# Who stores the moved squares of a hybrid attention layer, and a second place for them in the sparse branch

## The reference

```
h = rmsnorm(x, norm_g);  proj = h @ w_in          # (1024, 1024) @ (1024, 9.5 thousand columns)
ya = forgetting_attention(qa, ka, va, log_f) * silu(za)     # A: 8 heads, logits + c[t] - c[s], causal
yb = dsa_attention(qb, k, v, q_idx, k_idx, w_idx) * silu(zb)  # B: 8 heads share k and v; top 256 keys per query
yc = dilated_attention(qc, kc, vc) * silu(zc)               # C: 12 heads, windows with dilation 1, 4, 16
merged = sigmoid(ga) * (ya @ w_a) + sigmoid(gb) * (yb @ w_b) + sigmoid(gc) * (yc @ w_c)
out = rmsnorm(x + merged @ w_o, final_g)
```

## Time and profile before

| | before |
|---|---|
| time, median of 3 runs | 1370.05 us (1369.61 to 1372.65) |
| profiled execution, its own time | 1370.07 us |
| its span, first to last instruction | 1368.3 us |
| mean granted TensorE clock | 0.997 of full speed |
| TensorE busy | 1331.6 us (97%) |
| DVE, ACT, GpSimd busy | 771.8 (56%), 627.7 (46%), 297.3 us (22%) |

### The profile page before, as it was taken

How to read it: one execution, slowest core, us unless ns; L and a number is a source line. 1 busy time by engine, 2 the same in 40 slices (tenths; PEclk the granted TensorE clock), 3 DMA queues, 4 the chain that set the end, 5 groups by cost and what they waited for, 6 DMA issues and landing times.

```text
span 1368.3 us, 20758 instructions
## 1 busy us (share of the span) xinstructions
PE 1331.6 (97%) x7690; PEld 1084.3 (79%) x7690; DVE 771.8 (56%) x1716; ACT 627.7 (46%) x1381; POOL 297.3 (22%) x464
## 2 busy tenths in 40 slices
PE   7999999999999999999999899899999999999998
PEld 6988877777788888887778677777878788888886
DVE  6569866666766875575545454644444354223634
ACT  7467866666644541114343464544444322113223
POOL 3123111102103000005354412434342330000100
PEclk9999999999999999999999999999999999999999
DMA  7055222212214322225555423433443452321522
GB/s 223 23 139 131 63 69 63 63 44 66 70 42 124 91 68 79 81 78 156 151 144 161 137 86 94 120 83 92 133 140 100 145 155 62 84 78 62 185 92 101
DMA packets 124548, 139.54 MB, mean 102 GB/s; under 512 B 13888, under 2 KB 99520, under 8 KB 124192
## 3 DMA queue, kind: packets, MB, share of 16 engines
q0 software_dynamic: 26624, 80.00, 19.3%
q1 hardware_dynamic: 97824, 58.22, 15.7%
HBM read 99.95 MB, written 34.03 MB: 98 GB/s over the span
## 4 chain that ended last, share of the span: by engine, by line
PE 80%; DMA 7%; DVE 4%; POOL 4%; issue 3%; ACT 2%; POOLq 0%; ACTq 0%; DVEq 0%
PE bank L1120 20%; PE bank L1122 20%; PE bank L1121 20%; PE bank L1293 5%; DMA square_scratch<-pa 4%; PE slot L1254 4%; PE bank L1266 3%; PE slot L1120 2%; PE slot L1121 2%; PE slot L1122 2%; POOL ptsa L1038 2%; DVE idle_out L1673 1%; PE slot L1228 1%; DVE slot L1866 1%; DMA ptsb<-square_scratch 1%
## 5 line engine op out<-in xcount | busy, mean ns | idle before, releaser
L1120 PE MATMUL bank<-hs,w_hl 128*128 128x512 f32 x1088 | 432.7, 398 | 5.0 <-DVE qc L1809 2.9
L1122 PE MATMUL bank<-hs,w_hl 128*128 128x512 f32 x1088 | 424.6, 390 | 0.0
L1121 PE MATMUL bank<-hs,w_hl 128*128 128x512 f32 x1088 | 424.2, 390 | 0.0
L1120 PEld LDWEIGHTS bank<-hs,w_hl 128*128 128x128 f32 x1088 | 204.7, 188 | 50.6 <-issue 10.4
L1122 PEld LDWEIGHTS bank<-hs,w_hl 128*128 128x128 f32 x1088 | 204.5, 188 | 44.2
L1121 PEld LDWEIGHTS bank<-hs,w_hl 128*128 128x128 f32 x1088 | 204.9, 188 | 39.6
L1646 DVE TENSOR_TENSOR w_hl<-w_raw,w_hl 128x512 fp32r<-128x512 f32 (+1 forms) x168 | 113.3, 678 | 213.6 <-ACT w_hl L1357 212.0
L1357 ACT ACTIVATE w_hl<-w_raw 128x512 fp32r<-128x512 f32 (+1 forms) x168 | 104.0, 623 | 157.9 <-PE bank L1122 150.1
L1673 DVE TENSOR_SCALAR_CACHE_REDUCE idle_out<-score,state 128x768 uint8<-128x768 f32 (+3 forms) x140 | 115.4, 824 | 4.8
L1038 POOL DMA_DIRECT2D ptsb<-square_scratch x96 | 61.8, 650 | 119.9 <-PE bank L1293 96.0
L1866 DVE CUSTOM_DVE_ANT_0 slot<-slot,score 128x128 f32<-128x128 f32 (+5 forms) x64 | 47.0, 785 | 50.5 <-PE slot L1254 50.3
(11 more groups left out here) (337 smaller groups left out, 2439.1 us busy)
## 6 DMA issues: line engine op xcount, KB each, us to landing
w_raw<-in_w_in_dram SPq DMA_DIRECT2D x136, 256.0 KB, 2.9
merged_scratch<-ms POOLq DMA_DIRECT2D x16, 512.0 KB, 3.5
ms<-merged_scratch POOLq DMA_DIRECT2D x16, 512.0 KB, 4.1
square_scratch<-pb POOLq DMA_DIRECT2D x20, 256.0 KB, 2.9
ptsb<-square_scratch POOLq DMA_DIRECT2D x80, 64.0 KB, 2.3
xn<-in_x_dram SPq DMA_DIRECT2D x8, 512.0 KB, 6.8
iq_st<-iq_hl POOLq DMA_DIRECT2D x32, 128.0 KB, 2.8
w_raw<-in_w_o_dram SPq DMA_DIRECT2D x16, 256.0 KB, 3.3
```

What stands on the lines that cost most here:

```text
L1120: pe.matmul(out_, wh, mh, start=start, stop=False)
L1121: pe.matmul(out_, wh, ml, start=False, stop=False)
L1122: return pe.matmul(out_, wl, mh, start=False, stop=stop)
```

## The change

The store of a square is issued by ACT, behind the second exponential of the same run, with its two waits (for the transposition, and for the loads of two squares before). GpSimd keeps the four loads and the wait for the store. PTQ in B gets a second place, 512 columns of `c_tables`, so that the loads there too wait for PV of two squares back. The count of landed loads, `square_in`, is split into one for each parity of the square, and the waits on it are rewritten to match.

```diff
-                at = len(squares) - (2 if br == "a" else 1)
+                at = len(squares) - 2
...
-        PTQ = {"a": [at(k, f"ptsa{k}", [P, TB, P]) for k in (44, 76)], "b": [at(46, "ptsb", [P, 4, P])] * 2}
+        PTQ = {"a": [at(k, f"ptsa{k}", [P, TB, P]) for k in (44, 76)], "b": [at(46, "ptsb", [P, 4, P])]}
...
+        PTQ["b"].append(c_tables[:, 0:4 * P].rearrange("p (b c) -> p b c", c=P))
...
-        single_exp, squared, square_stored, square_in = sem("single_exp"), sem("squared"), sem("square_stored"), sem("square_in")
+        single_exp, squared, square_stored = sem("single_exp"), sem("squared"), sem("square_stored")
+        square_in = [sem(f"square_in{i}") for i in range(2)]
...
 # GpSimd, step "square"
-                    pool.wait_ge(squared, n + 1)
-                    if n >= 2:
-                        pool.wait_ge(square_in, 64 * (n - 1))
-                    pool.dma_start(mid[0:W // P].rearrange("b p c -> p b c"),
-                                   PR[br][:, 0, 0:W].rearrange("p (b c) -> p b c", c=P)).then_inc(square_stored, 16)
                     if a["before"] is not None:
                         full(pool, a["before"]["pv"])
                     pool.wait_ge(square_stored, 16 * (n + 1))
                     for j in range(4):
...
-                                       ).then_inc(square_in, 16)
+                                       ).then_inc(square_in[n % 2], 16)
...
 # TensorE, step "pv"
-                            pe.wait_ge(square_in, 64 * (a["square"] + 1))
+                            pe.wait_ge(square_in[a["square"] % 2], 64 * (a["square"] // 2 + 1))
...
 # ACT, at the end of step "exp"
+                    if a["dma"]:
+                        n, br, W = a["square"], a["br"], len(a["moved"]) * P
+                        act.wait_ge(squared, n + 1)
+                        if n >= 2:
+                            act.wait_ge(square_in[n % 2], 64 * (n // 2))
+                        act.dma_start(square_dram[n % 2][0:W // P].rearrange("b p c -> p b c"),
+                                      PR[br][:, 0, 0:W].rearrange("p (b c) -> p b c", c=P)).then_inc(square_stored, 16)
```

## The result

The changed kernel takes 1353.70 us (median of 4 runs, 1353.31 to 1354.19), the kernel before, beside it on the same chip, 1371.10 us (1369.61 to 1372.65). The ratio is 0.9873, 95% interval 0.9856 to 0.9890. The forecast was 1358.5 us with a range of 1354 to 1366, so the direction was right and the gain larger than forecast, by a little more than the range allowed.

What follows compares the result with a forecast made beforehand. TensorE, busy 1331.6 of 1368.3 us, was taken as the bound, leaving its idle time and lost clock to win. Gains 6.2 + 5.6 + 2.9 less 3.0 gave 11.7 us: 1358.5 us from 1370.07, range 1354 to 1366.

Steps and rivals of the forecast that it cites:

- Part 1: Stores leave GpSimd's queue, where loads stood ahead; TensorE's waits in A go: 6.2 us won.
- Rival (a): In A, stores lose in landing what they win in issue: 1364.6 us; chance 0.25 together with rival (d).
- Part 2: Start of B: first store no longer behind six share loads; less idle time, no low clock: 5.6 us won.
- The wait under "issue": TensorE's wait at the start of B, placed at 852.10 on the first product with moved blocks: 1.2 us, goes.
- The wait for yb: TensorE's wait at the start of B for the copy that frees a bank: 2.8 us, some 1.4 remain.
- The clock's 3.0 us: Start of B: granted clock no longer falls to 0.50, which cost half of 5.93 us of busy time.
- rival (d): Start of B: low clock stays, yb wait keeps its length: 1362.8 us; chance 0.25 together with Rival (a).
- Part 3: B: loads wait for PV of two squares back; four TensorE waits for loads go: 2.9 us won.
- Rival (b): Waits only move; yb copy, qa copies and ACT's issues eat the gain: 1370 us; chance 0.09.
- Part 4: ACT pays 0.37 us for each of 41 issues; TensorE sees a quarter to a fifth: 3 us lost.
- its lower bound, in brackets: ACT's cost per store issue could be 0: the sequencer might issue while the exponential still runs.
- Rival (c): ACT's issue is on the path, TensorE sees all 41: slower, 1388 us at GpSimd's 0.79 us; chance 0.05.

Runs made afterwards that it cites:

- Experiment 3: Changed kernel with ACT's stores in A only, B as in the kernel before: 1362.83 us, ratio 0.9951.
- experiment 9: Changed kernel, but in A GpSimd issues the stores, each ahead of the loads of the square before: 1353.11 us, ratio 0.9881.
- experiment 4: Changed kernel with only the first store of B back on GpSimd, behind the six loads of shares: 1359.27 us, ratio 0.9925.
- experiment 8: Changed kernel with ACT's store ahead of the second exponential instead of behind it: 1364.43 us, ratio 0.9968.
- experiment 5: Changed kernel with one more 8 KB DMA, which nothing waits for, issued by ACT behind each of 41 stores: 1355.86 us, ratio 0.9901.
- Experiment 1: Changed kernel with one place for the moved blocks of B, as before: 1356.76 us, ratio 0.9907.
- experiment 2: Second place for B alone, against the kernel before, stores still issued by GpSimd: 1366.85 us, ratio 0.9978.
- Experiment 10: Changed kernel with one extra 8 KB DMA per square issued by ACT right behind the first exponential: 1354.07 us, ratio 0.9883.
- Experiments 5 and 6: Changed kernel with one or three extra 8 KB DMAs issued by ACT behind each store: 1355.86 us with one, 1371.13 us with three.

## Why the prediction was wrong in size and right in kind

- **Part 1, 6.2 us in A: right, 6.8.** Experiment 3 gives 6.8 alone. The waits for the exponentials went, that for ptsa fell from 2.7 to 0.6. The prediction kept the landing at 5.3 us; landings fell by a quarter (4.7 to 3.5 us at 448 KB). It had named the loads ahead of the store as what counts, and experiment 9 shows just that; that the order alone, on GpSimd, does it was not among its theories. Rival (a), that what is won in issue is lost in landing, had the sign of this effect wrong.
- **Part 2, 5.6 us at the start of B: right, 6.15.** It was one store behind six loads (experiment 4 gives 5.6 to 6.0 by itself). The wait under "issue" went (it ends at 853.69; 852.10 is the start of the matmul ahead of it), and the granted clock is 1.00. The wait for yb fell from 2.8 to 0.6 us and not to 1.4. The clock's 3.0 us were sized right, and rival (d) is out. That the clock would not fall with 1.4 us of idle time left was argued from one row, where 2.7 us left it at 1.00; in experiment 8 it is low behind 2.0 us. So the row was no safe guide, though the conclusion held: in experiment 5 the yb wait is 1.3 us, and the clock shows no fall there.
- **Part 3, 2.9 us for the second place: right, about 3.** Experiment 1, without it, loses 3.0 us at two places. Behind the start of B TensorE gains 3.6 us in the changed kernel, 3.6 with the second place alone (experiment 2) and 0.6 with ACT's stores alone (experiment 1), so 0.6 of it comes with either.
- **Rival (b)**, that the waits only move, is out as well: between 625 and 1100 us one wait of TensorE is longer than before, and by 0.1 us.
- **Part 4, 3.0 us lost by ACT's 41 issues: the step that failed.** The term was mis-sized; it measures 0.1 us, the wait for qa at 633 us that grew from 0.66 to 0.75. "If a quarter to a fifth of the issues is seen by TensorE in full" took for granted that ACT itself loses 0.37 us at each store. The size was right (0.37 us in the trace), the loss was not: 36 of 41 issues lie in full under the exponential ahead and the read of its sum. Experiment 10 adds 41 issues in such a place and TensorE loses nothing by them; experiment 9 takes ACT's 17 issues in A away and gets back 0.1 us at qa. The prediction had this in its lower bound, in brackets, and then took the duration of an SP row for it and a share seen by TensorE that no row gave. It also held the 15.2 us against ACT's busy time in the 160 us of A, though A has only 17 of the 41 issues (6.2 us). Rival (c) rested on the same reading. Experiments 5 and 6 show the share for an issue that has no cover: a tenth of the first half microsecond a square, and more than the assumed quarter only of what comes on top.

Of the 4.8 us between 1358.5 and 1353.7, 3.0 are this term (the 0.1 us that it measures is inside the 6.8 of A). Another 1.8 come from the three gains, each 0.5 to 0.7 us better than taken. The range was too narrow at this end: with the better bound of every term the sum was 7.5 + 7.0 + 2.9 - 0 = 17.4 us, 1352.7, but the range stopped at 1354, with only 5 in 100 below 1355.

The Trainium skill, Advanced Engine Details and Errata, section Sequencer Loop, says that the sequencer pushes an engine instruction into a queue, in which that instruction waits for its semaphores. That it can then go on to a DMA behind it is a reading of that page, not its words. The row of 655.15 us agrees with it: the issue lies within the exponential of 654.60. With Part 4 at 0, the prediction's other terms give 1355.4. The Trainium skill, DMA: Bandwidth & Descriptors, section Issuing engines are not separate DMA queues, which the prediction did weigh, says that starting DMAs on several engines saves only the time to initiate them, and that this is usually small beside the DMA itself. For one store the traces agree: at 448 KB ACT's land in 3.5 us and GpSimd's of experiment 9 in 3.8, and an issue of 0.98 us stood against a landing of 4.7. What counted here is the sum of what stands ahead in the queue: four loads took 3.0 us to issue, six loads of shares 3.1.

Open: the rest of the idle time (2.9 us for qc in C; 0.7 for qa, 0.6 each for yb and ptsa) was not tried. Experiment 9's order was tried in A only: whether GpSimd with the first store of B ahead of the share loads would do as well as ACT is not known, since experiment 4 changed the place and the issuer of that store together. How the 11 us of experiment 8 divide between the wait and the visible issue is not told apart.

## What to carry to other kernels

Before moving a DMA to another engine, look at what stands ahead of it in its queue: one store behind six loads was worth 6 us, and where it was tried, putting the stores ahead of the loads on the same engine did as well as changing the engine. If the engine that takes it computes, put it right behind a long instruction of that engine whose inputs are long there, and with its own waits already met: here it then cost 0.1 us for 41 stores. Where nothing runs over it, the price grew faster than the delay: 41 delays cost 2.3 us at a median of 0.5 us each and 17.6 us at 1.5.

## What the runs showed of the hardware that was not expected

- A DMA issued by ACT took 0.37 us for 128-partition stores, and starts while the activation ahead of it in the list still runs. One of 16 partitions took 0.32 us right behind the first exponential (experiment 10) and 0.53 in the median right behind a store (experiment 5); which of the two, the running activation or the issue just ahead, makes the difference is not told apart.
- The landing of a store depends on what was issued just ahead: 448 KB took 4.7 us behind four loads from the same queue, 3.5 (ACT) to 3.8 us (GpSimd) ahead of them, and the loads of 112 KB then took 4.2 us instead of 2.7.
- The low clock (0.50, the level of 1.2 GHz) at the start of B stood behind two idle times of TensorE close together (1.2 and 2.8 us before, 2.1 and 1.9 in experiment 4), and is absent in the changed kernel, where 0.6 us is left of them. But two are not needed, and the length of an idle time alone doesn't tell: one of 2.0 us in experiment 8 was followed by 0.50, one of 2.7 us in the kernel before by 1.00.
